# Two chained transformer blocks on one core: queries behind the gathers, tile order and the feed-forward start

## The reference

```
# first layer
proj   = rmsnorm(x) @ w_in                    # 5376 columns: attention, gated scan, branch gates
merged = g0 * (attention @ w_up_att) + g1 * (bidirectional_scan @ w_up_hg)
x      = x + merged @ w_out
q      = rmsnorm(x) @ w_q                     # 8 heads x 2 x 128
v1,i1  = top_k(q_half0 . keys0, 16);  v2,i2 = top_k(q_half1 . keys1, 16)
top,idx = top_k(v1[i] + v2[j], 16)            # 16 of 128*128 experts for each head
x      = x + sum_k gelu(u[idx_k] . h) * softmax(top)_k * v[idx_k]   # 8*16 experts a token
x      = x + sigmoid(rmsnorm(x) @ ple_gate) * (p @ ple_proj)
# second layer; six rows of modulation come from silu(c) @ w_ada
h      = rms_norm(x) * (1 + sc_m) + sh_m
y      = concat(dilated_attention(h), sigmoid(og) * mlstm(h)) @ w_out
x      = x + gt_m * y
h      = rms_norm(x) * (1 + sc_f) + sh_f
x      = x + gt_f * (silu(h @ w_gate) * (h @ w_up)) @ w_down        # inner width 2816
```

## Time and profile before

| | us |
|---|---|
| median of 3 runs | 1446.43 |
| the three runs | 1443.64, 1446.43, 1447.96 |
| the profiled execution | 1444.79 |
| its span, first to last instruction | 1442.7 |
| PE busy / DVE / ACT / GpSimd in it | 1280.6 / 725.5 / 238.9 / 323.3 |
| mean granted TensorE clock | 0.958 |

### The profile page before, as it was taken

One profiled execution on the slowest core, in us unless ns is written; L12 is line 12 of the kernel. 1 busy time (PEld: TensorE's weight loads), 2 busy tenths in 40 slices (PEclk: granted clock), 3 DMA queues, 4 the chain that ended last, 5 costly groups with the idle time before them and its releaser, 6 DMA issues.

```text
span 1442.7 us, 12479 instructions
## 1 busy us (share of the span) xinstructions
PE 1280.6 (89%) x4494; PEld 731.9 (51%) x4494; DVE 725.5 (50%) x1752; ACT 238.9 (17%) x611; POOL 323.3 (22%) x273
## 2 busy tenths in 40 slices
PE   7999899988598888778799887878999898999998
PEld 6756455575354444333333333333465456888743
DVE  3664523177748776677786865653154342100001
ACT  2242221112101111111211112112112411000000
POOL 0100000024244444454445445450000000000000
PEclk9999999999899999999999999999999999999999
DMA  7434657269889999999999999995344712443531
GB/s 282 175 117 175 233 177 274 92 271 385 367 330 422 420 419 419 415 421 421 421 414 410 419 410 420 415 421 200 117 167 168 283 64 97 171 154 108 204 132 43
DMA packets 98380, 398.72 MB, mean 276 GB/s; under 512 B 6353, under 2 KB 9809, under 8 KB 65425
## 3 DMA queue, kind: packets, MB, share of 16 engines
q0 software_dynamic: 37376, 270.29, 45.4%
q1 hardware_dynamic: 60944, 127.65, 24.8%
HBM read 396.86 MB, written 1.05 MB: 276 GB/s over the span
## 4 chain that ended last, share of the span: by engine, by line
PE 56%; DMA 24%; DVE 15%; issue 2%; ACT 2%; POOL 1%; DVEq 0%; SPq 0%; ACTq 0%
DMA big<-in_peer_uv,idx_t 20%; PE ps L497 16%; PE ps L509 15%; PE ps L749 8%; DVE big L1738 6%; PE ps L972 5%; PE ps L716 3%; DMA wring<-in_w_in 2%; PE ps L686 2%; DMA wring<-in_peer_wq 2%; POOL big L1339 1%; PE ps L954 1%; PE ps L523 1%; PE ps L589 1%; ACT rows L1161 1%
## 5 line engine op out<-in xcount | busy, mean ns | idle before, releaser
L749 PE MATMUL ps<-big,rows 128*128 128x512 f32 x1024 | 489.3, 634 | 103.0 <-ACT rows L1161 102.8
L1339 POOL DMA_INDIRECT big<-in_peer_uv,idx_t x256 | 310.6, 1213 | 403.2 <-PE ps L749 337.8
L749 PEld LDWEIGHTS ps<-big,rows 128*128 128x128 f32 x1024 | 202.6, 203 | 372.0 <-issue 371.9
L1738 DVE CUSTOM_DVE_ANT_0 big<-big 128x1024 f32<-128x1024 f32 x256 | 307.6, 1225 | 157.1 <-DMA big<-in_peer_uv,idx_t 154.5
L497 PE MATMUL ps<-wring,big 128*128 128x512 f32 (+1 forms) x576 | 252.5, 596 | 12.1 <-DMA wring<-in_w_in 8.9
L509 PE MATMUL ps<-big,wring 128*128 128x256 f32 x960 | 210.4, 382 | 1.0 <-DVE big L1393 1.0
L509 PEld LDWEIGHTS ps<-big,wring 128*128 128x128 f32 x960 | 184.0, 192 | 27.2 <-issue 1.9
L497 PEld LDWEIGHTS ps<-wring,big 128*128 128x128 f32 x576 | 110.4, 195 | 142.8 <-issue 128.4
L1155 ACT ACTIVATE small<-small 128x4 f32<-128x4 f32 x64 | 13.2, 206 | 526.2 <-DVE small L1743 526.1
L1161 ACT ACTIVATE rows<-const,small 128x128 f32<-128x128 f32 x256 | 81.9, 391 | 19.2 <-DVE small L1747 18.6
L716 PE MATMUL ps<-big,wring 128*128 128x128 f32 x512 | 66.6, 288 | 17.0 <-DMA wring<-in_peer_wq 12.5
(11 more groups left out here) (237 smaller groups left out, 892.6 us busy)
## 6 DMA issues: line engine op xcount, KB each, us to landing
wring<-in_w_in SPq DMA_DIRECT2D x17, 2048.0 KB, 8.6
wring<-in_w_ada SPq DMA_DIRECT2D x12, 2048.0 KB, 8.4
wring<-in_w_gate SPq DMA_DIRECT2D x5, 2048.0 KB, 7.7
wring<-in_w_up SPq DMA_DIRECT2D x5, 2048.0 KB, 7.8
wring<-in_w_down SPq DMA_DIRECT2D x5, 2048.0 KB, 7.6
wring<-in_w_out SPq DMA_DIRECT2D x4, 2048.0 KB, 11.4
wring<-in_peer_wq SPq DMA_DIRECT2D x4, 2048.0 KB, 8.0
big<-in_peer_uv,idx_t POOLq DMA_INDIRECT x256, 12.2
```

The source lines that it names most:

```text
L749: last = nc.tensor.matmul(banks[h], diag[:, k % DIAGS, :], v_part[:, ring_at(k), h * 512:(h + 1) * 512], start=False, stop=(k % SLOTS == S ...
L1339: pool.indirect_dma_start(pair_ring[:, ring_at(k), :], None, a["peer_uv"], bass.IndirectOffsetOnAxis(idx_t[:, k:k + 1], 0))\
L1738: nc.vector.tensor_tensor_reduce(u_part[:, ring_at(k), :], u_part[:, ring_at(k), :], h_t[:, b, :], 1.0, 0.0, ALU.mult, ALU.add, a_dot[:, i ...
```

## The change

Five places are edited.

1. **Queries behind the gathers.** `QUERY_FROM` now starts (1, 0) at batch 1, (1, 1) at 5 and (0, 3) at 9 (before: 0, 9 and 4). The search for (0, 3) starts at batch 14 (before 12), that for (1, 0) at 20 (before 19). The first batch of experts is made ahead of the score of (0, 2) and of the turn of block 1, on PE and on ACT, and ACT's table load comes ahead of all these.
2. **The load of `w_up_hg`** is issued just ahead of `ada5` and no longer ahead of `in_g2`. `ada_rows` from 2 on lie elsewhere, and ACT no longer waits for `ada_col 7`.
3. **After the gathers** `in2_q` of block 0 is cut in two halves of four calls, with the turn `n3T` between them, and DVE scales block 1 for `n4T` ahead of moving `in2_k`.
4. **Middle of the second layer:** the tile `in2_og` comes ahead of `ada8` to `ada11`, and the products of these four and their rows come later.
5. **The feed-forward's start:** `out2_0` and `out2_1` are both made for block 0 first, `n5T` of block 0 is turned ahead of `out2_1` of block 1, and both `gate0` and `up0` are made block by block.

```diff
-    starts = {(0, 1): 0, (0, 2): 6, (0, 3): 12, (1, 0): 19, (1, 1): 26, (1, 2): 34, (1, 3): 42}
+    starts = {(0, 1): 0, (0, 2): 6, (0, 3): 14, (1, 0): 20, (1, 1): 26, (1, 2): 34, (1, 3): 42}
...
-QUERY_FROM = {0: (1, 0), 4: (0, 3), 9: (1, 1), 14: (1, 2), 19: (1, 3)}
+QUERY_FROM = {1: (1, 0), 5: (1, 1), 9: (0, 3), 14: (1, 2), 19: (1, 3)}
...
-    t += ada[8:10] + [("in2_og", KD, 512, "w_in_2", 0, 512 * 6)] + ada[10:12]
+    t += [("in2_og", KD, 512, "w_in_2", 0, 512 * 6)] + ada[8:12]
...
-        ada_rows = [at(big, 18944 + 512 * (i % 2), 512) for i in range(ADA_COLS)]
+        ada_rows = [at(big, (18944 if i < 2 else 16896) + 512 * (i % 2), 512) for i in range(ADA_COLS)]
...
-                if name == "in_g2":
+                if name == "ada5":
                     wait_product(sp, "a_Y", 1)
...
             banks = [reserved("experts", 0, h) for h in range(2)]
             residual(0, banks)
+            experts(0, banks)
+            score(0, 2)
+            turn_query(1)
+            wait_turned("n2T", [1])
...
             wait_turned("n4T", [0])
-            by_rows("in2_q", hT2, blocks=[0])
+            wt = tile("in2_q", KD, 512)
+            q_sums = reserved("in2_q", 0)
+            for c in range(4):
+                nc.tensor.matmul(q_sums, hT2[:, c, 0:P], wt[:, c, :], start=(c == 0), stop=False)
             pe.wait_ge(h_ready, 7)
             turn("n3T", h_t, [1])
...
             by_rows("in2_vm", hT2)
-            ada_part(8)
-            ada_part(9)
...
             by_rows("in2_og", hT2)
-            ada_part(10)
-            ada_part(11)
-            ada_row(8)
-            ada_row(9)
+            ada_part(8)
+            ada_part(9)
...
+            ada_part(10)
+            ada_part(11)
+            ada_row(8)
+            ada_row(9)
...
+            turn_cat(0)
+            by_rows("out2_0", hT2, blocks=[0])
+            by_rows("out2_1", hT2, blocks=[0])
+            turn_cat(1)
+            by_rows("out2_0", hT2, blocks=[1])
+            turn_fed(0)
+            by_rows("out2_1", hT2, blocks=[1])
+            wait_turned("n5T", [0])
...
+            fed_block("gate0", 0)
+            turn_fed(1)
...
+            fed_block("up0", 0)
+            wait_turned("n5T", [1])
+            fed_block("gate0", 1)
+            fed_block("up0", 1)
...
-                if b == 0:
-                    wait_product(act, "ada_col", 7)
...
             scale(2, 1)
+            turned("n3T", 1, h3T, lane[:, L_PLE:L_PLE + KD])
             qk_out("in2_q", 0)
-            turned("n3T", 1, h3T, lane[:, L_PLE:L_PLE + KD])
             ple_add(1, 0)
             ple_add(1, 1)
+            scale(3, 1)
             qk_out("in2_k", 0)
-
-            scale(3, 1)
```

More of the change, by code:

```diff
@@ L182, in product_list @@
     p += [("d_Y", 1)]
-    p += half("catT", 0) + [("out2_0", 0)] + half("catT", 1) + [("out2_0", 1)] + rows("out2_1") + turned("n5T")
-    for i in range(6):
+    p += half("catT", 0) + [("out2_0", 0), ("out2_1", 0)] + half("catT", 1) + [("out2_0", 1)] + half("n5T", 0)
+    p += [("out2_1", 1)] + half("n5T", 1) + cols("gate0") + cols("up0")
+    for i in range(1, 6):
         for n in (f"gate{i}", f"up{i}"):
@@ L818, in _ @@
             wait_turned("n4T", [0])
-            by_rows("in2_q", hT2, blocks=[0])
+            wt = tile("in2_q", KD, 512)
+            q_sums = reserved("in2_q", 0)
+            for c in range(4):
+                nc.tensor.matmul(q_sums, hT2[:, c, 0:P], wt[:, c, :], start=(c == 0), stop=False)
             pe.wait_ge(h_ready, 7)
             turn("n3T", h_t, [1])
+            begin("in2_q", 0)
+            for c in range(4, KD):
+                last = nc.tensor.matmul(q_sums, hT2[:, c, 0:P], wt[:, c, :], start=False, stop=(c == KD - 1))
+            last.then_inc(product_done, 1)
             wait_turned("n3T", [1])
```

99 lines of the change are left out of this document (49 added, 50 removed).

## The result

| | before | changed |
|---|---|---|
| median of the runs, us | 1445.49 (4 runs, 1443.64 to 1447.96) | 1411.55 (3 runs, 1411.05 to 1412.03) |
| profiled execution, us | 1444.8 | 1411.05 |
| its span, us | 1442.7 | 1409.0 |
| mean granted clock of the span | 0.958 | 0.964 |

The ratio is 0.9765, with a 95% interval of 0.9741 to 0.9789. The changed kernel is 33.9 us faster, 1.6 us from the forecast of 1410. A fourth execution of it took 7396.11 us, with a span of 7394.1 us at a granted clock of 1.00; it is left out of the median and the ratio as a slow run, and no trace shows what happened in it. In a later group of runs the changed kernel had 1411.72 beside 1441.46 (0.9795, 0.9781 to 0.9809), that is 29.7 us: it came out alike, and the kernel before 4 us quicker.

What follows compares the result with a forecast made beforehand. PE was taken to bound the stages before and after the gathers, the DMA engines the gathers. The terms sum to 35.8 us off 1444.8, 1409.0; half of the 1.6 us to the median added gives 1410 us, range 1402 to 1422.

Steps and rivals of the forecast that it cites:

- 1, `w_up_hg`: Before the gathers, at in_g2: PE's wait of 4.9 us and 2.3 us of low clock go, -7.2 us.
- 2, `g_OT`: At g_OT and the first lifted product: 1.4 us of gap and 1.0 of low clock go, -2.4 us (-1.4 to -4.1).
- 3, gathers: In the gathers: two holes in the DMA rate close, 12.2 and 2.1 us, -14.3 us (-10 to -15.3).
- 4, after the gathers: Behind the gathers: PE's waits of 1.15 us at n3T and 1.45 at n4T go, -2.6 us.
- 5, `in2_og` and `ada`: Second layer's middle: the wait and slow clock at in2_og go, a 3 us wait at ada11 comes, -2.0 us.
- 6, feed-forward's start: At gate0: waits of 3.62 and 2.49 us and 1.6 of clock go, up0 costs 0.4, -7.3 us (-9.3 to -4).
- the large hole: Window 390 to 410 us at 164 GB/s, put down to the load of peer_q3: 12.2 us missing, all to go.
- small hole: Window 330 to 350 us, at the first batch of experts: 3.1 us missing, 2.1 to be gained.
- no stretch under 400 GB/s: Sign to see in the trace after, for the gathers' first 100 us.
- a full spell of low clock: Case at the new wait for ada11: the clock falls for a full spell, +1.5 us instead of -2.0.
- The clock doesn't come back: Rival, chance 0.15: only the gaps close and slow spells move elsewhere, gain 27.4 us, 1418.
- The gathers don't fill up: Rival, chance 0.07: PE paces batches 1 to 12 or gathers come late; gathers' gain shrinks to about 3 us, 1421.

Runs made afterwards that it cites:

- e1: The kernel before with only the load of w_up_hg moved from ahead of in_g2 to ahead of ada5: 1434.4 us, ratio 0.9952.
- e2: The kernel before with only the gathers' change, both the queries' batch numbers and the earlier first batch of experts: 1431.1 us, ratio 0.9919.
- e12: The changed kernel run again, unchanged, in a later group: 1411.72 us, ratio 0.9795 to the kernel before.
- e7: The changed kernel with query (0, 3) from batch 5 and (1, 1) from batch 9: 1423.28 us, ratio 0.9862 to the kernel before.
- e8: The changed kernel with query (0, 3) from batch 6 and (1, 1) from batch 10: 1416.63 us, ratio 0.9809 to the kernel before.
- e3: The kernel before with only the queries' and searches' new batch numbers, the first batch of experts left as it was: 1432.3 us, ratio 0.9940.
- e5: The changed kernel with in_2's in2_og and the ada tiles and products back in their old order: 1412.02 us, ratio 0.9787 to the kernel before.
- edits 1 and 6: Against the kernel before, w_up_hg's load moved to just ahead of ada5, and the feed-forward's start reordered: 7.3 and 7.5 us gained in the pair.
- edit 5: Against the kernel before, tile in2_og loaded ahead of ada8 to ada11, whose products and rows come later: 2.9 us gained, then 1.6 lost, in the pair.
- edit 2: Against the kernel before, ACT no longer waits for ada_col 7 at the turns g_OT: 0.8 us gained in the pair.
- e9: The changed kernel with the product ada11 and rows 10 and 11 moved behind the attention's last product: 1404.91 us, ratio 0.9746 to the kernel before.

## Why the prediction was right, point by point

| step | forecast | in the pair | over all traces or by experiment |
|---|---|---|---|
| 1, `w_up_hg` | -7.2 | -7.3 | -7.0; e1 -6.9 |
| 2, `g_OT` | -2.4 | -0.8 | -2.1 |
| 3, gathers | -14.3 | -12.9 | e2 -11.7; in traces without the stall some -7 to -11 |
| 4, after the gathers | -2.6 | -3.0 | -3.0 |
| 5, `in2_og` and `ada` | -2.0 | -2.9, then +1.6 of clock | +1 |
| 6, feed-forward's start | -7.3 | -7.5 | -8.7 |
| sum | -35.8 | -33.7 with 0.9 ahead | e12 as a whole -29.7 |

The mechanisms of steps 1, 4 and 6 and of the large hole held; that the time came within 1.6 us of the forecast is in part luck. The kernel before was traced with a stall that step 3, in its small hole, took for an effect of the order, and in the group of e12, without the stall, the gain is 29.7 us and not 35.8.

**1** held in both of its halves, the gap and the clock. Nothing came late next.

**2** had the right mechanism, and in the pair too large a term. The gap of 1.4 closes (from the second turn's start to the first lifted product 1.75 us, before 2.88; over all traces 1.67 against 3.06). The share of the clock was taken as 1.0 with bounds 0 and 2.7. The first product begins in the low clock either way: from its start to the next it takes 5.7 to 6.5 us in the five traces without the edit, and 4.9 to 5.2 in six with it; the changed kernel's own trace, with 6.4, is the seventh and ate the term. The means differ by 0.7, so over all traces the step gives 2.1. The spell of low clock there is 6.8 us long in the five and in the seventh, and 3.4 us in the six.

**3** was right on the large hole and on its cause, which e7 and e8 show. The sum of 14.3 is at the upper end: the pair has 12.9, and e2, in a group without the stall, 11.7 (0.9893 to 0.9946 leaves room for 7.8 to 15.4). The step that failed is that of the small hole. I read the first experts' start at 331.90 as set by the order behind the last query, and it was set by a stall within that query. The forecast "first experts 4 us sooner counted from the first gather" came true in the pair (21.85 against 26.0), and is empty without the stall: e12 has 19.1, and e1 and e3, with the old order, 19.1. The hole of 1 us that was expected at the second batch isn't there (421 GB/s); one of 2 us at the fifth (the window of 327 GB/s) was not foreseen. Of the signs named, "no stretch under 400 GB/s" failed there, and the way from the first gather to the last became 12.9 us shorter and not 14 (687.1 and 674.2 when counted to the last batch's experts, an end 3 us behind that of the prediction's 684).

**4** was 0.4 better than forecast and came out the same in every trace: from the last batch's experts to `in2_if` 98.2 us in four traces without it (99.7 in e2), 95.0 to 95.4 in nine with it.

**5** is the term that, as far as the traces can tell, has the wrong sign. The wait moved as told: 2.96 us at `ada11` where 3 was forecast. In the pair it gave 2.9 us by the turns of block 1, near the -2.7 of its mechanism; that was luck, since the mean of the six traces with the edit is only 0.9 us under that of the six without (61.4 against 62.3), in three of them since the clock fell behind the wait, and since the kernel before's own trace, with 63.2, is at the long end of those without it (four of the six have 61.7 to 61.9). And the sum stopped at the turns. Behind them, DVE isn't sooner ready for `catT` by as much as PE is (2.34 us of wait in e12 where the kernel before had 1.57), and a low clock lies there for longer (10.2 us in the pair, 6.8 in e12, 3.4 in the kernel before and in e5). At +1 it ended near the bound of +1.5 that I had for "a full spell of low clock".

**6** was right on both waits, and the clock returned with them; it was undersized by 1.4 us. `up0` by block costs what the prediction took from the earlier trace rows: 192 matmuls in 21.60 us are 7.2 for 64, twice that is 14.4, against 14.0 for the wider calls. The rule on narrow calls ("TensorE: Matmul & The Clock Gate", Back-to-back issue gap, of the Trainium skill), by which, as an estimate, `up0` by block would have cost some 6 us more, isn't borne out by the trace for these float32 shapes (21.60 us for 192).

**The rivals.** "The clock doesn't come back" (1418) is refuted for edits 1 and 6 by the rows above, and holds for edit 5, and in the pair for edit 2. "The gathers don't fill up" did not happen: 421 and 417 GB/s stood in the two stretches of 100 us behind the queries.

```profile
400.00:500.00 100.00, 87.80 (x300) 47.57 (x301) 73.46 (x207) 16.87 (x55) 46.92 (x38) 0.97 1.01 421
500.00:600.00 100.00, 78.28 (x236) 39.66 (x235) 73.48 (x216) 15.51 (x51) 41.77 (x35) 0.91 1.02 417
```

In the pair the errors are 1.6 in step 2, 1.4 in step 3 and 0.7 in step 5, against 0.9 gained ahead of all edits and 0.7 in the others. Over all traces they are larger and cancel in part: step 5 is 3 too high and step 3 at least 2.6, step 6 1.4 too low. Two of the prediction's bounds don't follow from its own terms: these add up to 21.4 us at the low end, not 20, and `out2_0` without its wait of 0.78 and its slow 8.76 would be 2.4 us, not 1.9. Neither moves the forecast.

## To carry to other kernels

Among transfers that fill the DMA engines, place the first use of a tile by the time its load takes there (here 24 to 29 us, not the 8 us of a load alone), counted in batches of the work that frees the gathers' slots: one batch too few empties the queue, and the gain rises with each batch until the load is covered. A wait that you only push on to a later tile is worth what the next consumer makes of it; follow the sum to the end of the stage, not to the first point that comes sooner, and look whether the waiting step has a later place where another engine is waited for anyway (e9: 6.8 us). Before a hole is put down to the order of the work, look at what PE did in the 15 us ahead of it in the trace: a gap that nothing ends may belong to that group of runs and not to the order, and a change of the order is then at most an insurance against it.
